# The root of a norm taken out of the projection's operand and multiplied onto its results in PSUM

## The reference, cut to what matters

```python
def rmsnorm(x, g):
    y = x * lax.rsqrt(jnp.mean(x * x, axis=-1, keepdims=True) + EPS)
    return y * g

for i in range(DEPTH):                              # DEPTH = 2
    h = rmsnorm(x, ln1_g[i]) @ w_in[i]              # q, k, v of two attentions, c_q, c_kv, k_r, gate
    ...                                             # fox, diff and MLA attention
    x = x + jnp.concatenate([o_fox, o_diff, o_mla], axis=-1) @ w_o[i]
    up = causal_dwconv(rmsnorm(x, ln2_g[i]) @ w_up[i], conv_w[i], conv_b[i])
    g, u = up[..., :D_FF], up[..., D_FF:]           # D_FF = 2816
    x = x + (jax.nn.silu(g) * u) @ w_down[i]
```

## Time and profile before

| | us |
|---|---|
| median of three runs | 2513.49 |
| profiled execution, its own time | 2513.49 |
| its span | 2513.3 |
| PE busy | 2444.7 (97%) |
| DVE busy | 1288.1 (51%) |
| ACT busy | 1024.9 (41%) |
| POOL busy | 979.5 (39%) |

### The profile page before, as it was taken

One profiled execution on the slowest core, in us unless ns is written; L12 is line 12 of the kernel. 1 busy time (PEld: TensorE's weight loads), 2 busy tenths in 40 slices (PEclk: granted clock), 3 DMA queues, 4 the chain that ended last, 5 costly groups with the idle time before them and its releaser, 6 DMA issues.

```text
span 2513.3 us, 32865 instructions
## 1 busy us (share of the span) xinstructions
PE 2444.7 (97%) x12642; PEld 2038.2 (81%) x12642; DVE 1288.1 (51%) x2269; ACT 1024.9 (41%) x1795; POOL 979.5 (39%) x512
## 2 busy tenths in 40 slices
PE   9999999999999999999999999999999999899998
PEld 6986788888788778888888888888888888887766
DVE  3356589630235657984116742731372552556563
ACT  4465344432345645444334323231322332454552
POOL 3232356765432325576654223223222224222231
PEclk9999999999999999999999999999999999999999
DMA  4211245222321124532322111111121111111100
GB/s 173 72 55 68 93 159 193 96 98 95 105 84 55 34 81 151 196 134 99 109 93 68 51 51 51 59 53 65 51 68 43 51 51 51 62 51 35 34 17 34
DMA packets 54587, 200.52 MB, mean 80 GB/s; under 512 B 6176, under 2 KB 6176, under 8 KB 53664
## 3 DMA queue, kind: packets, MB, share of 16 engines
q1 hardware_dynamic: 52272, 189.27, 22.2%
q10 hardware_dynamic: 2160, 9.15, 1.0%
HBM read 196.29 MB, written 2.10 MB: 79 GB/s over the span
## 4 chain that ended last, share of the span: by engine, by line
PE 77%; DVE 16%; ACT 3%; POOL 2%; issue 2%; DVEq 0%; ACTq 0%; POOLq 0%
PE ps L907 25%; PE ps L574 18%; PE ps L594 16%; PE ps L624 7%; DVE arena L2007 7%; PE ps L1038 2%; PE ps L799 2%; DVE arena L2196 2%; DVE arena L2193 1%; DVE norm_sq L1971 1%; PE ps L1234 1%; POOL wl L2671 1%; PE ps L815 1%; POOL norm_acc L2684 1%; DVE hl L1983 1%
## 5 line engine op out<-in xcount | busy, mean ns | idle before, releaser
L2671 POOL TENSOR_TENSOR wl<-wring,wh 128x1024 fp32r<-128x1024 f32 (+1 forms) x305 | 771.9, 2531 | 1241.4 <-ACT wh L1274 1229.8
L1274 ACT ACTIVATE wh<-wring 128x1024 fp32r<-128x1024 f32 (+1 forms) x305 | 316.7, 1041 | 465.1 <-PE ps L907 229.6
L574 PE MATMUL ps<-hh,wh 128*128 128x512 f32 x768 | 299.8, 390 | 10.1 <-DVE hl L1983 5.1
L574 PE MATMUL ps<-hh,wl 128*128 128x512 f32 x768 | 299.0, 389 | 0.0
L574 PE MATMUL ps<-hl,wh 128*128 128x512 f32 x768 | 299.0, 389 | 0.0
L594 PE MATMUL ps<-hh,wh 128*128 128x512 f32 (+1 forms) x472 | 201.6, 427 | 4.9 <-DVE hl L2652 2.4
L594 PE MATMUL ps<-hh,wl 128*128 128x512 f32 (+1 forms) x472 | 188.2, 399 | 0.0
L594 PE MATMUL ps<-hl,wh 128*128 128x512 f32 (+1 forms) x472 | 187.8, 398 | 0.0
L2007 DVE CUSTOM_DVE_ANT_0 arena<-arena 128x1024 f32<-128x1024 f32 x96 | 182.6, 1903 | 8.6 <-DVE arena L2196 0.3
L574 PEld LDWEIGHTS ps<-hh,wh 128*128 128x128 f32 x768 | 144.1, 188 | 44.4 <-DVE hl L1983 5.0
L574 PEld LDWEIGHTS ps<-hh,wl 128*128 128x128 f32 x768 | 144.2, 188 | 30.2
(11 more groups left out here) (369 smaller groups left out, 5628.3 us busy)
## 6 DMA issues: line engine op xcount, KB each, us to landing
wring<-wts SPq DMA_DIRECT2D x290, 512.0 KB, 3.3
arena<-wts SPq DMA_DIRECT2D x48, 512.0 KB, 4.1
wring<-wts SPq DMA_DIRECT2D x16, 384.0 KB, 3.1
xL<-xt SPq DMA_DIRECT2D x4, 512.0 KB, 5.3
arena<-tab SPq DMA_DIRECT2D x1, 2048.0 KB, 15.5
arena<-cv ACTq DMA_DIRECT2D x2, 1024.0 KB, 5.4
arena<-tab ACTq DMA_DIRECT2D x1, 2048.0 KB, 7.7
out_t<-xL ACTq DMA_DIRECT2D x8, 256.0 KB, 2.1
```

The source lines that it names most:

```text
L574: mm = nc.tensor.matmul(o[0], a, b, start=start and k == first and j == 0, stop=stop and k == last and j == 2)
L1274: nc.scalar.activation(wh[:, sn % SPLIT_SLOTS, :kn * w], raw(u)[:, :kn * w], ACT.Copy).then_inc(act_done, tick("act", ("hi", u)))
L2671: G.tensor_tensor(wl[:, sn % SPLIT_SLOTS, :kn * w], raw(u)[:, :kn * w], wh[:, sn % SPLIT_SLOTS, :kn * w].bitcast(F32), ALU.subtract).then_inc(
```

## The change

The projections of the two norms in the first block now run on x times g. ACT writes its high part straight from x (`high_x`), DVE its low part (`low_x`), and neither waits for the root. The root's matmul moves behind `cq` (layer 1), behind `ckv` (layer 0) or behind the first up pair, and DVE multiplies the root onto the results where they lie in PSUM (`by_root`): the three `cn` tiles as they are copied, the `misc` bank, each of 12 key and query tiles, and each of 44 up tiles. For the values, which have positions on the partitions, PE transposes the root (four transposes) and ACT's copy out of PSUM scales with it. `first_norm` and all constant matmuls but 24 at the start go. The readers of these banks on ACT (`high_tile`, y(m)) now wait for DVE's multiply. The modulation's 96 reduces are spread over up tiles 0 to 30 (one or two per tile: 1, 2, 1, 2, ... up to tile 9, then 2, 1, 2, 1, ..., and from tile 21 on 2, 1, 2, 1, ... again; tiles 20, 21 and 29, 30 have two each) and stand ahead of the tile's conv; their scratch row goes to PSUM banks 0 and 1, and the up tiles use banks 2 to 5. SP loads x and the first weight units in turn.

```diff
@@ pe
-                if l:
-                    stir(7, 10)
-                    norm(("ln1", l))
-                    stir(6, 13)
-                else:
-                    first_norm(("ln1", l))
+                if l == 0:
+                    stir(6, 24, ones[:])
...
                 project(("cq", l), ...
+                if l:
+                    norm(("ln1", l))
...
                 if l == 0:
+                    norm(("ln1", l))
...
-                stir(7, 21)
-                norm(("ln2", l))
-                stir(6, 13)
...
                     project(("up", l, j), ...
+                    if j == 0:
+                        norm(("ln2", l))
@@ act
+            def high_x(tag, *tiles):
...
+                    nc.scalar.activation(hH[:, m, :], xL[:, m, :], ACT.Identity,
+                                         scale=col(tag[0], 8 * tag[1] + m)).then_inc(
...
                 split(("up", l, 1), first)
                 root(("ln2", l))
-                high(("ln2", l), hH)
...
-                        act.wait_ge(pe_done, at("pe", "up", l, m))
+                        act.wait_ge(dve_done, at("dve", "us", l, m))
@@ dve
+            def low_x(tag, *tiles):
...
+                    V.scalar_tensor_tensor(out=hLo[:, m, :], in0=xL[:, m, :], scalar=col(tag[0], 8 * tag[1] + m),
+                                           in1=hH[:, m, :].bitcast(F32), op0=ALU.mult, op1=ALU.subtract).then_inc(
...
+            def by_root(x, rs, *key):
+                V.tensor_tensor(x, x, rs, ALU.mult).then_inc(dve_done, tick("dve", key))
...
+                dve.wait_ge(act_done, at("act", "rstd", ("ln1", l)))
                 for m in range(3):
                     dve.wait_ge(pe_done, at("pe", "cn", l, m))
-                    V.tensor_copy(cn[:, m, :], ps[:, m, :]).then_inc(dve_done, tick("dve", ("cn", l, m)))
+                    V.tensor_tensor(cn[:, m, :], ps[:, m, :], rs1x, ALU.mult).then_inc(dve_done, tick("dve", ("cn", l, m)))
                 dve.wait_ge(pe_done, at("pe", "misc", l))
+                by_root(ps[:, 3, :], rs1x, "mis", l)
...
                 for m in range(2 * FT):
+                    y, u = yb[:, m % 3, :], ps[:, up_bank(m), :]
+                    dve.wait_ge(pe_done, at("pe", "up", l, m))
+                    by_root(u, rstd, "us", l, m)
+                    for x in range(min(48, 48 * m // ADA_TILES), min(48, 48 * (m + 1) // ADA_TILES)):
+                        modulate(l, x // 2, x % 2)
                     dve.wait_ge(act_done, at("act", "y", l, m))
...
-                    if m < 24:
-                        modulate(l, m)
@@ pool
                 if l == 0:
                     split(("cq", l))
-                split(("ckv", l))
+                    accumulate(("ln1", l), 1, 2, 3)
+                    split(("ckv", l), slice(0, 1))
+                    accumulate(("ln1", l), 4, 5, 6, 7)
+                    split(("ckv", l), slice(1, 2))
+                else:
+                    split(("ckv", l))
```

More of the change, by code:

```diff
@@ L87, in weight_jobs @@
             add(("up", l, j), "w_up", l, 0, KT, [(256 * j, 256)])
[L88 to L89 removed]
+            for i, after in enumerate(ADA_JOBS):
+                if after == j:
+                    add(("ada", l, i), "ada_w_2", l, 0, KT, [(256 * i, 256)])
         for j in range(4):
@@ L170 @@
 TAB3 = 640 + 512 + 256
-ARENA = 25680
+ARENA = 25728
+ADA_TILES = 31
+ADA_JOBS = [(9 * i) // 7 + 2 for i in range(12)]
 def dense(s, t):
@@ L633, in stir @@
                     nc.tensor.matmul(ps[:, b, 0:128], by, by, start=True, stop=True)
[L635 to L643, removed]
             def norm(tag):
@@ L707, in _ @@
                     chain(ps[:, h, :], [(idn[0:4, h:h + 1].to_broadcast([4, P]), fgc[0:4, :])], ("cb", l, h))
+                claim([4], "dve", "rsc", l)
+                pe.wait_ge(act_done, at("act", "rstd", ("ln1", l)))
+                for t in range(NT):
+                    last = nc.tensor.transpose(ps[:, 4, 128 * t:128 * t + 128], rs1x[:, 128 * t:128 * t + 128], idn)
+                last.then_inc(pe_done, tick("pe", ("rsc", l)))
                 tile_part("q", 0, 5, 0, KT)
@@ L1329, in _ @@
             for l in range(DEPTH):
-                if l == 0:
-                    for m in range(KT):
-                        act.wait_ge(x_loaded[m // 2], 16)
-                        nc.scalar.activation(x_sq[:, m, :], xL[:, m, :], ACT.Square).then_inc(
-                            act_done, tick("act", ("sq", ("ln1", l), m)))
-                    split(("cq", l), slice(0, 1))
-                    act.wait_ge(prm_loaded, 16)
-                root(("ln1", l))
                 if l:
                     act.dma_start(arena[:, 0:TAB1], tab1).then_inc(tab1_loaded, 16)
-                    high(("ln1", l), hH)
                 else:
-                    high(("ln1", l), hH, tiles=range(0, 2))
+                    act.wait_ge(prm_loaded, 16)
+                    high_x(("ln1", l), 0, 1)
+                    split(("cq", l), slice(0, 1))
+                    high_x(("ln1", l), 2, 3, 4, 5)
                     split(("cq", l), slice(1, 2))
-                    high(("ln1", l), hH, tiles=range(2, KT))
+                    high_x(("ln1", l), 6, 7)
+                    square_x(0, 1, 2, 3)
+                    split(("ckv", l), slice(0, 1))
+                    square_x(4, 5, 6, 7)
                     nc.scalar.activation(fgn[:, 0:8], col("fin", 0, 8), ACT.Square).then_inc(act_done, tick("act"))
@@ L1356, in _ @@
                 nc.scalar.activation(lamc[:, 2:4], lamc[:, 0:2], ACT.Exp).then_inc(act_done, tick("act", ("lamexp", l)))
-                split(("ckv", l))
+                first, second = slice(0, 1), slice(1, 2)
+                if l:
+                    split(("ckv", l), first)
+                split(("ckv", l), second)
+                split(("k", l, 0))
+                root(("ln1", l))
                 square(("cq", l), 0, ("cn", l))
                 square(("cq", l), 1, ("cn", l))
-                split(("k", l, 0))
-                first, second = slice(0, 1), slice(1, 2)
                 def high_tile(x, n, b):
-                    act.wait_ge(pe_done, at("pe", x, l, n))
+                    act.wait_ge(dve_done, at("dve", x + "s", l, n))
                     if x == "k" and n >= 2:
@@ L2099, in follow1 @@
                 def follow1(s):
+                    for x, n, c, m in pieces_of(s):
+                        if x != "v" and c + m == KT:
+                            scale_tile(x, 2 * (s // 16) + n, 6 if x == "k" else 7)
                     if s in LOW_STEPS:
```

90 lines of the change are left out of this document (66 added, 24 removed).

## The result

The changed kernel takes 2523.22 us (median of five runs, 2520.14 to 2525.68) against 2513.49 before: 1.0037 of it, 95% interval 1.0025 to 1.0050. It is 9.7 us slower where 6.4 less was forecast; the time lies at the top of the range, on the wrong side. The profiled execution has a span of 2520.9, 7.6 over the one before, and that difference is explained here. In the page's busy times PE does 18 us less than in the earlier trace rows, DVE 63 more.

A forecast was written before the change was run, and what follows sets the result against it. PE, busy 97% of the span, was taken as the bound. Terms -6.8 - 13.2 - 8.75 + 2 x 9.7 + 2 x 1.5 = -6.35 us took 2513.3 to 2507.0, range 2488 to 2524.

The forecast's parts named there:

- Part 5: Attention: roots on eleven key and query tiles ahead of ACT's read, mostly hidden; loss 1.5 us a layer.
- signs of being wrong: Up pairs 24 to 31 keep 10.9 us, the multiply takes over .95, or pair 1's low parts come in time.
- Parts 2 and 3: Second norm in two layers, gain 6.6 us each; layer 1's first norm, gain 8.75, as PE's waits go.
- Part 1: Start of layer 0: first product and gate matmuls come earlier, with new waits; gain 6.8 us.
- the new wait: Up pair 1, second norm: PE waits 3.1 us for the second unit, split behind root, table load and Silu.
- the terms that the text adds up to 28.9: Start: POOL's queue until the low part of ckv's second unit is done, making PE wait 2.5 us.
- Part 4: Up stage: the helpers' loop outgrows PE's pace, mainly in the gate pairs; loss 9.7 us a layer.
- The step-through of the helpers' order: Up stage: helper work followed in order gives 11.3 to 11.5 us a pair, gate pairs 12.9 to 13.1.
- B: Up stage gives little back, reduces and low parts meeting less or PSUM scratch easing exclusion; 2484 to 2498 us, chance .20.
- C: Root's multiply in PSUM is dear, up stage and attention, deciding from about .95 us; 2519 to 2535, chance .15.
- D: Slow stretches of the clock move, or attention costs its 4.5 us; 2510 to 2522 us, chance .15.

The follow-up runs named there:

- e9: Changed kernel with the root's multiply of the ten key and query tiles per layer between attention steps on one column in place of 512; 2521.92 us.
- e1: Changed kernel without the root's multiply on the ten key and query tiles per layer projected between attention steps; 2508.93 us.
- e2: Changed kernel with the root's multiply of a step's key or query tile issued on DVE right behind that step's score; 2519.8 us.
- e10: Changed kernel without the root's multiply on the 44 up tiles, ACT waiting for PE as before the change; 2506.02 us.
- e6: Changed kernel with ACT's split of up pair 1's second unit ahead of the second norm's root, table load and large Silu; 2525.06 us.
- e7: Changed kernel with the first query tile projected ahead of the four gate matmuls, its split moved ahead of the root; 2526.22 us.
- e8: Changed kernel with five mends: early root, up split ahead of root, query tile ahead of gate, early POOL low part, new reduce table; 2508.26 us.
- e11: e8 with early root for query tiles only, first value tile's split and large Silu reordered, ckv norm later, another reduce table; 2500.87 us.

## Why the prediction was wrong

**Part 5, the attention, failed, and with it the sign.** It put 1.5 us a layer on the eleven roots and 4.5 as the upper bound; 6.3 and 8.9 were measured, 12.2 of the 14 us between sum and result. (Half the length of eleven roots is 11 x .36 = 4.0, so the bound itself was .5 too high.) The reason in the text was ".72 ahead of ACT's read. Most steps have room." The instruction was priced, at its true length (.69), and the wait was put at nothing: the trace of before shows DVE's chain, ACT's copy and DVE's low part at the place near 190, and the copy beside the chain. With the new wait the copy starts when DVE's queue has come to the root. e9 shows that most of the cost is this wait, e1 its size (14.3 us over both layers), e2 that with the root early in DVE's queue the low part waits for nothing at the query tile. PE's waits in the attention add up to 13.1 and 13.2 us in the two layers, against 8.3 and 8.4 before. The rest of 6.3 and 8.9 goes with the lower clock, which lay 2.1 and 8.9 us longer on these stages than before; a run that keeps the clock up with the waits in place was not made. None of the prediction's signs of being wrong looked at the attention.

**Parts 2 and 3 held, and Part 1 down to the gate.** The second norm gave -10.7 and layer 1's first norm -10.0 against -8.75, and it was 3.6 for the root's matmul and the new wait against 4.1. The start's times were met within .7 us down to the gate, though the terms that the text adds up to 28.9 make 28.65 (29.55 was measured). There the eight gate matmuls took 6.50 in place of 4.55, as the lower clock began .8 us behind their start in place of 2.7, and the transposes cost .77 in place of .45, so that 4.5 of 6.8 was left.

**Part 4, the up stage, held:** 8.8 against 9.7 a layer, with gate pairs at 12.70 (12.9 to 13.1) and the pairs of tiles 10 to 19 at 11.26 (11.3 to 11.5). The step-through of the helpers' order gave each of these. What it left out is the clock behind the last wait of 3.2, at its lower level for 3.4 us: 1.7 a layer. e10 shows the part of the root in it: without it nearly all of the loss goes.

**The rivals.** B is out: the up stage lost 8.8 a layer, and a reduce beside POOL still takes 2.2 to 3.1 in the changed kernel with its scratch row in PSUM. C fell too, though the time lies in its range: the multiply in PSUM takes .69. It decided from .95 on. What came is D's second half, "attention costs its 4.5", at well over its bound, and slow stretches: added up over the trace, 74 us at the lower clock in place of 54. That the stated range still holds 2523 is luck: its top was there for C and D, and the time is C's by number only and above D's 2522.

## What to carry to other kernels

When a step moves to another engine, price the wait that it puts on its reader before its own time: name what stands ahead of it in its engine's queue, and what the reader did meanwhile that now comes afterwards. A wait that is removed by splitting one unit earlier shows up at the next unit unless everything behind the same blocker moves; e6 and e7 gained nothing alone, and only the sets of mends (e8 and e11) beat the kernel before.

## What the runs showed of the hardware that was not expected

The granted clock fell to its lower level behind a wait of PE of 3.2 us in the attention (192.3 to 199.1) and behind the last wait of the up stage, also 3.2 (499.5 to 502.9). But the slow stretch at the gate's matmuls of 4 rows stayed at 10.2 us with the wait ahead of them gone (e7), only later. And a DVE instruction of two SBUF inputs on one column per partition took 1.93 us in place of .22 while POOL made a low part beside it, as it did before the change (1.98). It ends at 191.40, POOL's low part (189.05, 2.34 long) at 191.39, and all eight rows of that line which overlap a POOL row end .01 to .02 behind it: even so small an instruction waited for POOL's to end.
